# Four query tiles of the last score stage split in two, with the first part ahead of the third block's turn

## The reference

```python
x = x + gt1 * (merged @ lp['w_out'])
h2 = rmsnorm(x, lp['norm_ffn']) * (1 + sc2) + sh2
x = x + gt2 * peer(h2, ...)

def peer(h, w_query, sub_keys, expert_u, expert_v):
    q = jnp.einsum('btd,dhk->bthk', h, w_query).reshape(B, T, PEER_HEADS, 2, PEER_DKEY // 2)
    s = jnp.einsum('bthpk,hpnk->bthpn', q, sub_keys)
    sv, si = lax.top_k(s, PEER_TOPK)
    ...
    act = jax.nn.gelu(jnp.einsum('nd,ned->ne', hx, expert_u[ix]))
    return jnp.einsum('ne,ned->nd', act * gx, expert_v[ix])
```

## Time and profile before

| what | value |
|---|---|
| median of 3 runs | 4627.2 us |
| the profiled execution's own time | 4624.79 us |
| its span | 4623.0 us |
| PE (TensorE matmul) busy | 4462.3 us, 97% |
| DVE (VectorE) busy | 3094.3 us, 67% |
| POOL (GpSimd) busy | 1482.4 us, 32% |
| ACT (ScalarE) busy | 593.3 us, 13% |
| DMA over the span | 359 GB/s read from HBM and written |

### The profile page before, as it was taken

One profiled execution on the slowest core, in us unless ns is written; L12 is line 12 of the kernel. 1 busy time (PEld: TensorE's weight loads), 2 busy tenths in 40 slices (PEclk: granted clock), 3 DMA queues, 4 the chain that ended last, 5 costly groups with the idle time before them and its releaser, 6 DMA issues.

```text
span 4623.0 us, 60331 instructions
## 1 busy us (share of the span) xinstructions
PE 4462.3 (97%) x25249; PEld 3285.4 (71%) x25249; DVE 3094.3 (67%) x4135; ACT 593.3 (13%) x1161; POOL 1482.4 (32%) x1047
## 2 busy tenths in 40 slices
PE   7989999999999998999999999999999999999997
PEld 2776446445885444466555445799999999999997
DVE  1455518897997774247777587978855558886556
ACT  1530001432431000000000010100000000000001
POOL 0110002673334643103544244433322223322221
PEclk8999999999999999999999999999999999999999
DMA  9939988995448989987999987599999999999998
GB/s 396 405 124 379 375 336 348 390 409 233 140 142 313 408 350 408 385 334 304 421 420 420 411 317 298 225 377 419 419 420 419 408 406 421 418 420 418 403 420 334
DMA packets 237322, 1663.40 MB, mean 360 GB/s; under 512 B 28230, under 2 KB 32728, under 8 KB 37786
## 3 DMA queue, kind: packets, MB, share of 16 engines
q0 software_dynamic: 129616, 936.57, 49.9%
q1 hardware_dynamic: 99348, 677.25, 36.6%
q10 hardware_dynamic: 8088, 45.73, 2.5%
HBM read 1639.68 MB, written 18.94 MB: 359 GB/s over the span
## 4 chain that ended last, share of the span: by engine, by line
PE 39%; DMA 8%; DVE 7%; issue 1%; POOL 1%; ACT 0%; ACTq 0%; DVEq 0%; POOLq 0%
PE ps L249 26%; PE ps L2737 12%; DMA arena_sb<-peer_v,arena_sb 7%; DVE arena_sb L447 3%; PE ps L2679 1%; POOL arena_sb L396 0%; DMA x_rows<-arena_sb 0%; DVE arena_sb L2426 0%; DVE arena_sb L2436 0%; DVE arena_sb L2428 0%; DVE arena_sb L2433 0%; DVE arena_sb L2423 0%; DVE arena_sb L2509 0%; DVE arena_sb L2464 0%; DVE arena_sb L2455 0%
## 5 line engine op out<-in xcount | busy, mean ns | idle before, releaser
L249 PE MATMUL ps<-arena_sb 128*128 128x224 f32 (+3 forms) x9728 | 2292.8, 396 | 8.4 <-ACT arena_sb L2237 2.6
L249 PEld LDWEIGHTS ps<-arena_sb 128*128 128x128 f32 x9728 | 1670.7, 192 | 614.2 <-issue 327.8
L447 DVE SCALAR_TENSOR_TENSOR arena_sb<-arena_sb 128x2048 f32<-128x2048 f32 x412 | 986.6, 2395 | 473.8 <-DMA arena_sb<-peer_v,arena_sb 442.9
L442 DVE CUSTOM_DVE_ANT_0 arena_sb<-arena_sb 128x2048 f32<-128x2048 f32 x416 | 975.5, 2359 | 326.7 <-DMA arena_sb<-peer_u,arena_sb 326.5
L396 POOL DMA_INDIRECT arena_sb<-peer_v,arena_sb x416 | 606.9, 1459 | 1135.6 <-DVE arena_sb L447 929.4
L396 POOL DMA_INDIRECT arena_sb<-peer_u,arena_sb x416 | 628.6, 1511 | 924.1 <-DVE arena_sb L442 571.6
L2737 PE MATMUL ps<-arena_sb 128*128 128x224 f32 x4096 | 776.5, 353 | 1.3 <-ACT arena_sb L2776 0.7
L2737 PEld LDWEIGHTS ps<-arena_sb 128*128 128x128 f32 x4096 | 774.4, 190 | 2.2 <-issue 1.0
L1949 PE MATMUL ps<-arena_sb 128*128 128x512 f32 x768 | 338.7, 599 | 15.0 <-DMA arena_sb<-w_gb_r 7.4
L1949 PEld LDWEIGHTS ps<-arena_sb 128*128 128x128 f32 x768 | 144.7, 191 | 203.4 <-issue 181.3
L2132 PE MATMUL ps<-arena_sb 128*128 128x512 f32 x640 | 275.8, 593 | 3.1 <-DMA arena_sb<-w_out 1.9
(11 more groups left out here) (329 smaller groups left out, 2871.4 us busy)
## 6 DMA issues: line engine op xcount, KB each, us to landing
arena_sb<-peer_ut SPq DMA_DIRECT2D x128, 1024.0 KB, 9.3
arena_sb<-peer_vt SPq DMA_DIRECT2D x128, 1024.0 KB, 9.3
arena_sb<-w_mod POOLq DMA_DIRECT2D x61, 1024.0 KB, 9.3
arena_sb<-w_qkv SPq DMA_DIRECT2D x48, 1024.0 KB, 9.2
arena_sb<-w_out SPq DMA_DIRECT2D x48, 1024.0 KB, 6.9
arena_sb<-w_query SPq DMA_DIRECT2D x48, 1024.0 KB, 7.1
arena_sb<-w_mod SPq DMA_DIRECT2D x35, 1024.0 KB, 8.9
arena_sb<-w_ga_r SPq DMA_DIRECT2D x32, 1024.0 KB, 8.4
```

Of the source, the lines that this page charges most:

```text
L249: mm = pe.matmul(out, weights[:, k * P:(k + 1) * P], x[:, k, :], start=(k == 0), stop=(k == chunks - 1))
L442: nc.vector.tensor_tensor_reduce(rows, rows, total, 1.0, 0.0, ALU.mult, ALU.add, seg.dots[:, p:p + 1]).then_inc(t.rows_used, 1)
L447: nc.vector.scalar_tensor_tensor(out=total, in0=rows, scalar=seg.weight[:, p:p + 1], in1=total, op0=ALU.mult, op1=ALU.add).then_inc(t.rows ...
```

## The change

1. On TensorE, in `expert_input` for the rest, ahead of the third block's transposes: after eight copies (blocks 0 and 1 are in h2t) it runs query tiles 0 to 3 on the first 256 tokens, into banks 4 to 7. In `scores` these four tiles then run on the last 128 tokens only. The later twelve tiles are as they were.
2. On ScalarE the spills come first, then the four copies of block 0, then the root of the last block, then the copies of block 1 and of block 2.
3. On VectorE six of the twelve rows come ahead of the wait for the spill.

GpSimd's program is not touched. SP's isn't either.

```diff
@@ expert_input
     def _(act):
-        t.root(act, nb - 1)
+        if nb == 1:
+            t.root(act, 0)
         for b in range(nb):
             act.dma_start(t.x_rows[g.first + b], x[:, b]).then_inc(t.x_spilled, 16)
         for b in range(nb):
+            if b and b == nb - 2:
+                t.root(act, nb - 1)
             for k in range(4):
...
         for b in range(nb):
+            if b == 2:
+                pe.wait_ge(copied, 8)
+                for n in range(EARLY):
+                    tile_full(pe, t, n)
+                    project(pe, t.ps[:, 4 + n, 0:2 * P], tile_slot(t, n), h2t[:, :, 0:2 * P])
             for k in range(KD):
@@ scores
+    early = EARLY if nb == 3 else 0
+    query_bank = lambda n: 4 + n if n < early else n % q_banks
...
         for n in range(tiles):
-            after(pe, query_done, n - q_banks + 1)
-            tile_full(pe, t, n)
-            project(pe, t.ps[:, n % q_banks, 0:nt], tile_slot(t, n), h2t).then_inc(t.tile_done, 1)
+            if n < early:
+                tile_full(pe, t, n)
+                project(pe, t.ps[:, 4 + n, 2 * P:nt], tile_slot(t, n), h2t[:, :, 2 * P:nt]).then_inc(t.tile_done, 1)
+            else:
+                if n >= early + q_banks:
+                    pe.wait_ge(query_done, n - q_banks + 1)
+                tile_full(pe, t, n)
+                project(pe, t.ps[:, n % q_banks, 0:nt], tile_slot(t, n), h2t).then_inc(t.tile_done, 1)
...
-            nc.scalar.activation(query[n % 2], t.ps[:, n % q_banks, 0:nt], ACT.Copy).then_inc(query_done, 1)
+            nc.scalar.activation(query[n % 2], t.ps[:, query_bank(n), 0:nt], ACT.Copy).then_inc(query_done, 1)
...
+        ahead = 6 if nb == 3 else 0
+        use_rows(dve, nc, t, behind[0][:ahead])
         dve.wait_ge(t.x_spilled, 16 * (NB - 1 + g.first + nb))
-        use_rows(dve, nc, t, behind[0])
+        use_rows(dve, nc, t, behind[0][ahead:])
```

More of the change, by code:

```diff
@@ L39 @@
 M_VECTOR = range(6, 12)
+EARLY = 4
 PICKS = P
```

## The result

| | before | changed | |
|---|---|---|---|
| median, 7 runs each | 4626.8 us | 4652.0 us | ratio 1.0048, 95% interval 1.0038 to 1.0059 |
| lowest, highest | 4617.9, 4640.0 | 4644.3, 4656.6 | |
| profiled execution, span | 4623.0 us | 4650.1 us | own time 4624.8 and 4652.0 us |

The change makes the kernel slower, by 25 us by the medians and by 22 us by the ratio (18 to 27 by its interval; the ratio is taken over all runs and is not the quotient of the two medians, here and in the table of the experiments). The forecast was +15, 4642, with 4651 as the upper end of the range; the measured median is 1 us above that end, and 1.0048 of 4627.2 would be 4649.

A forecast was written before the change was run, and what follows sets the result against it. VectorE's chain, fed by row DMAs, was taken as nearly the bound. Its first top comes 17.1 us later, less 2.1 us caught up in the experts, gives +15.0 us: median 4642.2, range 4632 to 4651.

The forecast's parts named there:

- The mechanism: GpSimd issues row 3 only after the twelfth copy, which early tiles delay; VectorE's late searches then hold TensorE; +15.0 us.
- Early start: TensorE's first query tiles start at about 2771.6 instead of 2777.27, 5.7 us won there.
- Split: Query tiles split into early and late parts cost 10.45 us instead of 10.32, 0.5 us for four.
- Twelfth copy: ScalarE's last copy of the third block stands at 2805.5, where it stood at 2777.2.
- Landing of the fourth row: Row 3's DMA, issued at 2806.4, lands in 7.4 us, bounds 4.8 and 9.9; the row starts at 2813.8.
- Rows 0 to 2: Issued in the stage before, usable at once by VectorE; their 3 x 2.45 us leave the stretch behind the spill.
- The pace: VectorE's rows from the fourth to the twelfth follow at 3.24 us each, as before, bounds 2.5 and 3.6.
- first top: VectorE's first search behind the twelve rows comes at 2842.0 against 2824.95, 17.1 us later.
- The last score: TensorE's scores wait for banks VectorE reads; it reaches the experts at 2968.3 instead of 2956.42, 11.9 us later.
- catching up in the experts: At the gate VectorE regains one tile's time, 2.1 us of the 17.1; as rival, with quick refill, chance 0.20.
- quick refill: Four rows issued in a burst, row chain only 8.5 or 11.1 us late; total +6 to +9, 4634; shared chance 0.20.
- The faster rival: Rows 3 to 5 available ahead of the early part's end, hot up to 10 us earlier; -5 us, 4622; chance 0.06.

The follow-up runs named there:

- rows_free: The changed kernel with GpSimd issuing the first twelve rows and four behind them ahead of its wait for the twelfth copy; 4616.4 us against 4629.9 before, ratio 0.9974.
- late_rows: The kernel before, with GpSimd also waiting, behind the twelfth copy, until ScalarE has copied the second query; 4638.8 us against 4630.4, ratio 1.0018.
- act_order: The kernel before with only the new ScalarE order (spills, copies of block 0, last root, other copies); 4624.3 us against 4630.4, ratio 0.9984.
- no_early: The changed kernel without its early query tiles, keeping ScalarE's order and six rows ahead; 4621.0 us against 4629.9 before, ratio 0.9984.

## Why the prediction was right or wrong

- **The mechanism** (GpSimd's wait, not in the diff, moved by the early part; the rows behind it; the searches; the scores' banks; the gate) is shown, by rows_free, which takes it away, and late_rows, which makes it alone.
- **Early start**: 11.3 us after the first turn forecast, 11.0 measured. **Split**: nearly free as forecast: two late tiles take 7.41 us.
- **Twelfth copy**: forecast 45.2 us after the first turn, measured 41.5. The 3.1 us for a low clock were not due: 128 instructions in 27.7 us, and the clock granted at 1.00 in the window shown.
- **Landing of the fourth row**: 7.4 us forecast, 5.4 measured (2811.18 to 2816.62). The Trainium skill's fit, an estimated 4.4 us (DMA: Bandwidth & Descriptors, Anatomy of one DMA), was 1.0 under it; the shortest row of a busy stretch was 2.0 over it. "No row DMA here was under 7.4" holds for that stretch only: ahead of 1500 us the trace of before has one of 5.7.
- **Rows 0 to 2** "can be used at once": each was waited for (1.53, 3.77 and 1.63 us), the third was used 24.4 us after the first turn, and VectorE stood 21 us ahead of the fourth and not some 30. This cost nothing, as the fourth came later still.
- **The pace, the term that failed**: "I keep 3.24, with 2.5 and 3.6 as bounds". It was 4.23, above the upper bound, 8 us from the fourth row to the twelfth. The text named the cause, three tiles asking for successors within 12 us, and yet gave it no price. With -3.7 at the twelfth copy, -2.0 at the landing and +7.9 at the pace the errors leave +2.2: first top 19.3 us late against 17.1. That it came so near is luck.
- **The last score**: TensorE was expected to stand before scores 8, 12, 14 and 15. It stood 7.13 us before score 4 first, a stop that the forecast didn't have, and before 8, 12, 14 and 15 as forecast; 14.9 us late against 11.9.
- **"I take 2.1 us" of catching up in the experts** did not come by the gate: it is late by 19.8, more than the top. 1.2 us of it are gone at the end of the span.
- **The sum**: +18.6 by the count from the first turn, +25 in the first medians and +22 against the later medians of before (4629.9, 4630.4 and 4628.2). The rest between 18.6 and 22 to 25 lies in front of the change or in the scatter. Kernels with early tiles have their first turn at 2765.8 on the mean of six profiles, those without at 2762.8; with a spread of 9 us, 6.4 of it between two profiles of one kernel, that neither shows nor excludes a cost there. It stays open.
- **The rivals**: quick refill, the rival with most of the remaining chance, had the landing right and the pace wrong. The faster rival, rows truly ahead, was priced at -5 (4622); made real it gives -9.3 and -11.1 by the traces and 4616 to 4618. Part of this is part 2's, to which the forecast gave nothing: alone it gives -4.9 by the trace (act_order).

## What to carry to other kernels

Before work is put ahead of a step, list every engine that waits for that step, those too whose code the diff doesn't touch: one semaphore (here the twelfth copy) may guard both a scratch area and, by mere program order, a stream of DMAs that needs no guard. Move the stream in front of the wait first; then the early work cost nothing here. And a stream that restarts after a pause meets whatever else was held back by the same pause: price it with those loads in it, not at its old pace.

## What the hardware showed that I had not expected

- In DMA engines that stood idle a row landed in 5.4 us; one issued 8 us later, with three rows in front of it and tile loads beside it, took 18.57 us (the chain above), the engines moving 420 GB/s.
- ScalarE's order alone, the spills and four copies moved ahead of one square root, gave 6 us. The spills, issued 4.4 us earlier, let VectorE start 6.5 us earlier (act_order). The last turn is no longer held up by the banks, and the first tiles start 2.4 to 2.9 us earlier and take 3.0 us less over two tiles (20.91 us in both no_early and act_order).
- The low clock did not vanish in act_order but stood elsewhere: the granted clock was 0.50 from 2770 to 2776 us there and back at full before the tiles, and in before it was 0.50 from 2774 to 2782 (a part of that is in the earlier trace rows). So the third turn paid, 3.83 us instead of 2.71:

```profile
2772.14 3.83 PE L2256 MATMUL ps<-ident_sb,arena_sb 128*128 128x128 f32 x16 [0.36 <-DVE arena_sb L2054]
```

How much of the gain is the clock's is not fixed: late_rows has the turns and copies of before, and its first two tiles took 22.43 us, not 23.94.
